# Modulation sums along the row: weights laid out turned, one accumulating VectorE operation for each 128 columns, no TensorE products

## The reference, cut to what matters

```
# block 1: six vectors of 1024
mod = silu(c) @ mod_w[0] + mod_b[0]
sh1, sc1, g1, sh2, sc2, g2 = split(mod, 6)
h = rms_norm(x, norm1_g) * (1 + sc1) + sh1
x = x + g1 * hybrid_mixer(h, ...)
...
# block 2, layer i in 0, 1: nine vectors of 1024, from two conditions (c for the tokens, c_ctx for the context)
m_l = (silu(c)     @ mod_w_2[i] + mod_b_2[i]).reshape(9, 1024)
m_c = (silu(c_ctx) @ mod_w_2[i] + mod_b_2[i]).reshape(9, 1024)
h + 0.5 * m[base + 2] * swiglu(rms_norm(h, g) * (1 + m[base + 1]) + m[base], w13, w2)
```

## Time and profile before

| | |
|---|---|
| median of 3 runs | 2817.83 us (2816.88 to 2820.12) |
| span of the profiled execution | 2811.8 us |
| PE busy | 2709.9 us (96%) |
| DVE busy | 2100.9 us (75%) |
| ACT busy | 1575.8 us (56%) |
| DMA | 776.11 MB, mean 276 GB/s |
| chain that ended last | PE 82%, DVE 11%, issue 3%, ACT 3% |

### The profile page before, as it was taken

How to read it: one execution, slowest core, us unless ns; L and a number is a source line. 1 busy time by engine, 2 the same in 40 slices (tenths; PEclk the granted TensorE clock), 3 DMA queues, 4 the chain that set the end, 5 groups by cost and what they waited for, 6 DMA issues and landing times.

```text
span 2811.8 us, 43791 instructions
## 1 busy us (share of the span) xinstructions
PE 2709.9 (96%) x17682; PEld 2472.9 (88%) x17682; DVE 2100.9 (75%) x1766; ACT 1575.8 (56%) x1410; POOL 0.4 (0%) x6
## 2 busy tenths in 40 slices
PE   6999999999999999999998999999989999999998
PEld 5889888888888888888886999999879999999998
DVE  6347649999999999999998787785545866754553
ACT  0045318888888888888884443353434434432442
POOL 0000000000000000000000000000000000000000
PEclk9999898999999999999998999999999999999999
DMA  9744448999999999999995876776317767754561
GB/s 391 255 164 135 151 171 329 381 380 388 389 385 392 390 390 393 394 390 382 386 379 199 297 251 255 258 266 243 142 65 251 283 222 262 270 178 165 165 194 62
DMA packets 172691, 776.11 MB, mean 276 GB/s; under 512 B 12272, under 2 KB 38000, under 8 KB 121616
## 3 DMA queue, kind: packets, MB, share of 16 engines
q1 hardware_dynamic: 168640, 768.71, 72.3%
q10 hardware_dynamic: 3920, 5.49, 0.7%
HBM read 773.10 MB, written 1.05 MB: 275 GB/s over the span
## 4 chain that ended last, share of the span: by engine, by line
PE 82%; DVE 11%; issue 3%; ACT 3%; DMA 0%; SPq 0%; DVEq 0%; ACTq 0%
PE psum L1257 38%; PE psum L1635 18%; PE psum L1211 7%; DVE w_low L2353 6%; PE psum L1675 4%; PE psum L1612 2%; PE psum L1653 2%; PE psum L1336 2%; ACT w_high L929 1%; PE psum L1355 1%; PE psum L1397 1%; PE psum L1492 1%; DVE arena L2380 1%; PE psum L1445 1%; PE psum L1520 1%
## 5 line engine op out<-in xcount | busy, mean ns | idle before, releaser
L2353 DVE TENSOR_TENSOR w_low<-ring,w_high 128x2048 fp32r<-128x2048 f32 x396 | 885.1, 2287 | 31.6 <-ACT w_high L929 20.5
L929 ACT ACTIVATE w_high<-ring 128x2048 fp32r<-128x2048 f32 x396 | 736.2, 1905 | 47.9 <-PE psum L1635 47.9
L1072 ACT ACTIVATE w_high<-ring 128x2048 fp32r<-128x2048 f32 (+1 forms) x199 | 362.4, 1829 | 561.2 <-PE psum L1257 478.0
L2489 DVE TENSOR_TENSOR w_low<-ring,w_high 128x2048 fp32r<-128x2048 f32 (+1 forms) x199 | 432.7, 2184 | 320.3 <-ACT w_high L1072 317.4
L1257 PE MATMUL psum<-h_high,w_high 128*128 128x256 f32 x2080 | 588.5, 283 | 21.6 <-ACT h_high L1085 20.4
L1257 PE MATMUL psum<-h_high,w_low 128*128 128x256 f32 x2080 | 590.6, 284 | 0.0
L1257 PE MATMUL psum<-h_low,w_high 128*128 128x256 f32 x2080 | 588.2, 284 | 0.0
L1257 PEld LDWEIGHTS psum<-h_high,w_high 128*128 128x128 f32 x2080 | 399.6, 192 | 24.1 <-issue 22.2
L1257 PEld LDWEIGHTS psum<-h_low,w_high 128*128 128x128 f32 x2080 | 394.9, 191 | 0.0
L1257 PEld LDWEIGHTS psum<-h_high,w_low 128*128 128x128 f32 x2080 | 394.5, 190 | 0.0
L1635 PE MATMUL psum<-w_high,xg 128*128 128x512 f32 x1056 | 296.0, 402 | 0.6 <-ACT xg L957 0.6
(11 more groups left out here) (288 smaller groups left out, 3441.5 us busy)
## 6 DMA issues: line engine op xcount, KB each, us to landing
ring<-in_exp_w SPq DMA_DIRECT2D x396, 1024.0 KB, 8.7
ring<-in_ffn_w SPq DMA_DIRECT2D x135, 1024.0 KB, 5.3
ring<-in_mod_w SPq DMA_DIRECT2D x96, 1024.0 KB, 5.6
ring<-in_ffn_w SPq DMA_DIRECT2D x40, 768.0 KB, 4.7
ring<-in_w_in SPq DMA_DIRECT2D x24, 1024.0 KB, 8.9
ring<-in_even_w_in SPq DMA_DIRECT2D x12, 1024.0 KB, 7.2
ring<-in_conv_w_in SPq DMA_DIRECT2D x12, 1024.0 KB, 5.1
ring<-in_w_branch SPq DMA_DIRECT2D x6, 1024.0 KB, 5.5
```

The costliest lines, as they stand in the source:

```text
L929: act.activation(high_ap(j, D), slot_ap(PLAN.moe_slot + j), ACT.Copy).then_inc(sem("expert_high_ready" + c.x), 1)
L1072: act.activation(high_ap(m, cols), slot_ap(s, 2, cols), ACT.Copy).then_inc(sem("w_high_ready"), 1)
L2353: dve.tensor_tensor(low_ap(PLAN.moe_slot + j, D), slot_ap(PLAN.moe_slot + j), high_ap(j, D).bitcast(F32), ALU.subtract).then_inc(sem("expe ...
L2489: dve.tensor_tensor(low_ap(s, cols), slot_ap(s, 2, cols), high_ap(m, cols).bitcast(F32), ALU.subtract).then_inc(sem("w_split"), 1)
```

## The change

- The host lays `mod_w` and `mod_w_2` out turned (`mods`): in a slot, partition p holds 1024 weights of output column 128 k + p, for two values of k. What is summed now lies along the row. A slot is contiguous in memory, 8 KB for each partition; before it was two pieces of 4 KB.
- The condition is no longer one number for each partition but a row of 1024 on every partition: a new tile `cond_rows` (3 x 1024), which the host hands over already repeated over the 128 partitions. ScalarE loads the first row (0.5 MB) at the start, ahead of `vecs`, and the other two (1 MB) later, and applies Silu in place.
- A block is one `scalar_tensor_tensor` of weights times the row, with the accumulated sum written to one column of `mod1` or `mod2`. The product itself goes over the weights, or to a scratch tile `mod_junk` (bf16) when a second condition still needs them.
- `mod_sum` and its psum units are gone, and so are `mod_sums` and `modulation` as a separate step: bias and gain follow directly behind the group's last slot. `gains2`, which used a tile of `mod_sums`, lies in a free piece of the arena.

```diff
@@ def mod_slot(i) @@
-                for k in (2 * pair, 2 * pair + 1):
-                    for c in range(conds):
-                        part = mod_sums[:, MOD_BUFFERS[n][c], :]
-                        cond = cs[:, k:k + 1] if block_ == 1 else cs2[:, k, c:c + 1]
-                        if k == 0:
-                            last = dve.tensor_scalar(part, w[:, k % 2, :], cond, None, ALU.mult)
-                        else:
-                            last = dve.scalar_tensor_tensor(part, w[:, k % 2, :], cond, part, ALU.mult, ALU.add)
-                        if (k % 2, c) != (1, conds - 1):
+                rows = (0,) if block_ == 1 else (1, 2)[:conds]
+                for j in range(2):
+                    k = 2 * pair + j
+                    for c, row in enumerate(rows):
+                        sums = mod1[:, g, k:k + 1] if block_ == 1 else mod2[:, layer, g, k, c:c + 1]
+                        to = w[:, j, :] if c == conds - 1 else mod_junk[:, :]
+                        last = dve.scalar_tensor_tensor(to, w[:, j, :], 1.0, cond_rows[:, row, :], ALU.mult, ALU.mult,
+                                                        accum_out=sums)
+                        if (j, c) != (1, conds - 1):
                             steps.done(last)
-                    if k % 2 == 0:
+                    if j == 0 and conds > 1:
                         steps.settle()
                 last.then_inc(sem("mod_slots_used"), 1)
-                dve.wait_ge(sem("mod_slots_used"), i + 1)
                 if pair == 3:
-                    dve.sem_inc(sem("mod_partials"), 1)
+                    steps.settle()
+                    dve.wait_ge(sem("mod_slots_used"), i + 1)
+                    modulation(n)
+                elif conds > 1:
+                    dve.wait_ge(sem("mod_slots_used"), i + 1)
@@ the program of ScalarE @@
+            act.dma_start(cond_rows[:, 0, :], ins["cond_rows"][0]).then_inc(sem("cond_landed"), 16)
             act.dma_start(vecs[:, 0:FIRST_VECS], ins["vecs"][:, 0:FIRST_VECS]).then_inc(sem("vecs_landed"), 16)
             act.dma_start(ones, ins["consts"][:, 0:P]).then_inc(sem("ones_landed"), 16)
+            act.wait_ge(sem("cond_landed"), 16)
+            act.activation(cond_rows[:, 0, :], cond_rows[:, 0, :], ACT.Silu).then_inc(sem("cond_ready"), 1)
...
+            act.dma_start(cond_rows[:, 1:3, :], ins["cond_rows"][1:3].rearrange("c p k -> p c k")).then_inc(
+                sem("cond2_landed"), 16)
...
+            act.wait_ge(sem("cond2_landed"), 16)
+            act.activation(cond_rows[:, 1:3, :], cond_rows[:, 1:3, :], ACT.Silu).then_inc(sem("cond_ready"), 1)
@@ the program of TensorE @@
-            def mod_sum(n):
-                conds = MODS[n][3]
-                u = U[mod_unit(n)]
-                pe.wait_ge(sem("mod_partials"), n + 1)
-                open_unit(pe, u)
-                for c in range(conds):
-                    for j in range(DC):
-                        at = j * conds + c
-                        mm = pe.matmul(unit(u)[:, at:at + 1], mod_sums[:, MOD_BUFFERS[n][c], j * P:(j + 1) * P],
-                                       ones[:, 0:1], start=True, stop=True)
-                mm.then_inc(psum_full, 1)
@@ the host @@
+    def mods(w):
+        t = w.reshape(w.shape[0], D, -1, DC // 2, 2, P)
+        return t.transpose(0, 2, 3, 5, 4, 1).reshape(w.shape[0], -1, DC // 2, P, SLOT)
```

More of the change, by code:

```diff
@@ L173, in gemm @@
     def gemm(self, name, tensor, index, k_chunks, col0, cols, n_units, mods_every=0, mods_end=0, split=False,
-             first=0, sums=True):
+             first=0):
         self.unit(name, n_units)
         self.slots[name] = []
-        before = self.n_mod_slots
         for k in range(0, k_chunks, 2):
@@ L195, in gemm @@
                 self.since_mods = 0
-        self.mods_after[name] = [n for n in range(len(MODS)) if sums and before < 4 * n + 4 <= self.n_mod_slots]
-        for n in self.mods_after[name]:
-            self.unit(mod_unit(n))
     def piece(self, name, z):
@@ L260, in make_plan @@
             p.unit("branch_turn2")
-        p.gemm(f"branch{b}", "w_branch", b, 4, 0, D, 2, mods_every=1, mods_end=L1_MODS, sums=False)
+        p.gemm(f"branch{b}", "w_branch", b, 4, 0, D, 2, mods_every=1, mods_end=L1_MODS)
     p.gemm("w_out", "w_out", 0, DC, 0, D, 2, mods_every=1, mods_end=L1_MODS)
@@ L331, in make_plan @@
     return p
[L334 to L348, removed]
-GAIN2_BUFFER = [b for b in range(MOD_SUMS) if b not in MOD_BUFFERS[L1_MODS]][0]
 PLAN = make_plan()
@@ L2188, in _ @@
                     soft(s + 1)
-                if s >= 2:
-                    for n in mods_ending(*ATT_MOD_SLOTS[s - 2:s]):
-                        modulation(n)
                 attended(s)
@@ L2201, in _ @@
             dve.sem_inc(sem("branches_ready"), 1)
-            for n in mods_ending(*ATT_MOD_SLOTS[-3:-1]):
-                modulation(n)
             def mods_of(name):
@@ L2230, in _ @@
                             link(last)
-                for n in PLAN.mods_after[f"branch{br}"]:
-                    modulation(n)
             def add_to(dst, name, gate):
@@ L2367, in squared_gains @@
                     gain = vec("final1")[:, k:k + 1]
-                    last = dve.tensor_scalar(mod_sums[:, GAIN2_BUFFER, k * P:(k + 1) * P], ones, gain, gain, ALU.mult, ALU.mult)
+                    last = dve.tensor_scalar(gains2[:, k * P:(k + 1) * P], ones, gain, gain, ALU.mult, ALU.mult)
                 link(last)
-                link(dve.tensor_scalar(mod_sums[:, GAIN2_BUFFER, :], mod_sums[:, GAIN2_BUFFER, :], 1.0 / D, None, ALU.mult))
+                link(dve.tensor_scalar(gains2, gains2, 1.0 / D, None, ALU.mult))
             def experts(c, steps, last=False, over=False):
@@ L2510, in norm2 @@
                      mod2[:, layer, 3 * which, :, t])
-            def modulations_of(name):
-                for n in PLAN.mods_after[name]:
-                    modulation(n)
             def ffn(e, layer, which, between=None):
```

82 lines of the change are left out of this document (19 added, 63 removed).

## The result

The changed kernel takes **2767.3 us** (median of 4 runs, 2760.8 to 2768.3) against 2817.4 us (median of 4, 2813.5 to 2820.1). The ratio is 0.9824, with a 95% interval from 0.9806 to 0.9842. The forecast was 2783 us with a range from 2774 to 2794. The direction was right, the gain of 50 us lay 15 us over the 35 I had worked out, and the range did not hold it. The profiled execution went from a span of 2811.8 us to one of 2759.0.

What follows compares the result with a forecast made beforehand. TensorE, busy 96% of the span, was taken to bound the kernel, with VectorE idle time in block 2. Terms summed to -34.6 us: span 2811.8 to 2777, median 2817.8 to 2783 us, range 2774 to 2794.

Steps and rivals of the forecast that it cites:

- Block 2, -33.5: Groups 8 to 23: TensorE's sums and a 0.84 us psum wait go, giving -33.5 us.
- Group 6, -3.4: Behind attention: transposes start earlier, -5.4 us, but branch 0 runs longer at half clock, +2; together -3.4.
- The start, +1.6 and +0.5: Up to z0: later landings and dearer VectorE operations, +1.6 us; a longer half-speed stretch for z0, +0.5.
- The price of the operation: VectorE's new modulation operation: 1.25 us in a row plus 0.1 for the accumulator read, 1.35 us.
- z0 to z2 -3.7: Sums behind z0 and z1 go, -3.4 us, and behind z2 -0.3; together -3.7.
- attention +1.3: All of attention: dearer VectorE slots on the chain, net of group 5's sum and bias, +1.3 us.
- Group 7, 0 and +0.7: Behind norm(1): removing the sum gains 0; a longer idle stretch can drop the clock earlier, +0.7 us.
- the seam, +1.9: Seam to block 2: group 8's slot ahead of the norm takes 5.4 us instead of 3.9; +1.9 us in all.
- The median: Whole kernel: the median of the runs lies 6.0 us above the profiled span, turning 2777 into 2783 us.
- The third: Rival, whole kernel: more gain, with landings not delayed, accumulator free and clock up no later; 2775 us or less; 9%.
- The half rate: Rival: VectorE's accumulating operation runs at half rate, some 2.4 us each, ending at 2826 us, slower; 4%.
- Second: Rival: cover the sums gave VectorE and ScalarE is lost, half of block 2's gain returns, +17, 2800 us; 8%.

Runs made afterwards that it cites:

- first pair: Original profiled traces laid side by side: the kernel before, span 2811.8 us, and the changed kernel, span 2759.0 us.
- second pair: Later traces of the same two kernels, both unchanged: the kernel before, span 2815.9 us, and the changed kernel, span 2764.5 us.
- after_third: The changed kernel run again, unchanged, on the chip of the kernels with filler products: 2765.0 us, ratio 0.9797 to the kernel before.
- op_twice: Changed kernel plus, ahead of each modulation operation, a second of the same size without the sum: 2885.8 us, ratio 1.0256 to the kernel before.

## Why the forecast was too high, step by step

The step that failed is TensorE's clock. In the sum it stands as a loss of 3.2 us (+0.5 at z0, +2 at branch 0, +0.7 at group 7), and in block 2 at nothing. It was a gain: the low stretches of the two traces of the kernel before sum to 143 and 151 us, those of the changed kernel's three to 113, 129 and 130, which is 13 to 38 us less, each worth half where TensorE is the bound. In the first pair it is 30 us less: 15 gained at most where I had 3.2 lost, and the span fell 18.2 us more than forecast. In the second pair it is 22 less: 11 at most, and the span fell 16.8 more. Some of that is chance, as the pairs of the table show; what stands behind block 2's sums is not. The other terms that were off are the price of VectorE's operation and the 0.09 us of TensorE for each vector.

- **Block 2, -33.5: right in mechanism, mis-sized.** In the first pair a vector taken away gives 1.79 us, and two give 3.58; I had read 1.70 and 3.49 from start to start. With the wait of 0.84, which went as forecast, the 16 sums are 34.9 us. The other 2 us of the first pair and 8 of the second are the clock: I wrote of it only at the start and behind attention, and never asked which low stretches of block 2 stood behind a sum. Of the second pair's 8 us a part is chance: between two traces of one kernel single low stretches come and go.
- **Group 6, -3.4: where it failed most clearly.** I wrote that the sum "also carried the clock up". It was the other way: with the sum's narrow products the clock stayed down, and in the changed kernel's three traces it is not low here at all. I also misread the length: I took the clock to rise at 328.2, the end of my window, but the next window of the same trace is low too, and the rise is at 330.7. And the transposes don't wait for VectorE's last product, as I had it: in the changed kernel they start at 315.49, and VectorE's last product runs from 316.22 to 316.64. So taking the sum away gave 6.75 us of the first pair and not 5.4, and branch 0 at full speed another 1.2, where I had subtracted 2. In the second pair, where the clock fell later in the sum, it was 4.2 and 2.2. The next window of the kernel before:

```profile
328.20:331.00 2.80, 2.80 (x15) 2.77 (x14) 2.76 (x4) 1.10 (x2) 0.00 (x0) 0.54 0.00 0
```

- **The start, +1.6 and +0.5: wrong in sign.** The operation at 1.15 in place of 1.35 gives 2.0 us over the ten behind the fourth slot; that slot began at 18.11, not 18.6; and the clock rose at 38.3, 3.4 us after z0's start, where before it was 5.4. From the reciprocal to the `tensor_scalar`, 3.13 in the forecast, it was 3.17.
- **The price of the operation.** I took the read for 0.1 us on top of 1.25. It lies beside the next operation, and the operation took 1220 ns where the old one took 1284 (why it is shorter no run separates). My lower bound of 0 for the read was the right end, and still too dear.
- **z0 to z2 -3.7 and attention +1.3** were right: -3.7, and +0.1 and +1.8 in the two pairs.
- **Group 7, 0 and +0.7, and the seam, +1.9.** Group 7's products cost nothing, as forecast. The seam's slot took 4.8 us (1505.70 to 1510.52), against 3.96 before and the 5.4 forecast. The 0.7 for the clock did not come.
- **The median.** I took it for 6.0 us above the span. What lies outside the span is 1.8 us (2760.8 against 2759.0); the rest was that the profiled execution, of either kernel, was the shortest of its four. Forecast and result are both of medians, so it did not move the miss.
- **The rivals.** The third ("the clock up no later at either place", at most 2775) is nearest to what happened, though the fourth slot did begin 0.8 us later; I gave it 9%. The half rate did not come. By the rule of the Trainium skill that I named beside it ("Vector Engine (DVE) Microarchitecture Reference", section 7) the operation would be at half throughput; measured is 1220 ns, full rate, and 1223 without the sum, so the trace contradicts the rule for this form. But the price I gave that rival was wrong by a factor of almost three: `op_twice` is 2886 us, not 2826. The change stood nearer to a loss than I said. Second, no cover was given back: TensorE's waits for VectorE's low parts in all of `after_third` are 1.4 us.

## What to carry to other kernels

On a kernel that TensorE bounds, ask of every short group of narrow products what it does to the clock behind it, not only how long it takes: here 41 us of products were worth 49, give or take 4. Slack on another engine is to be counted in the stretch where the new work stands and not over the stage: 317 us of idle time looked ample, 39.5 were free where the work was thickest, and an operation twice as dear would have made the change a loss. Where TensorE waits in any case, products without use that end before the wait does can keep its clock up, worth 14 to 18 us here, with an uncertainty of some 8.

## What I had not expected of the hardware

- The accumulated sum of a VectorE operation adds nothing to its duration: 1220 to 1225 ns with it and 1223 without. The read of 83 ns lies beside the next operation, and it is 1.15 us from start to start. How closely the operations without the sum would follow one another was not measured.
- Products of one and of 128 columns take the same time (3.6 and 3.7 us for 16 products), and the clock falls behind 16 narrow ones though TensorE is never idle: 7 to 20 us of low clock in the first part of block 2 against none, and 6.5 us of the whole time.
- The low stretches behind block 2's second and third sum of two vectors stand in all five traces with narrow products there, the one behind the first in four; single ones in the mixture of experts come and go.
